# One query pass for all 256 tokens and 156 instead of 152 dense columns in a two-layer expert kernel

## The chip, the cores and the metric

The kernel runs on one core of a Trainium2 chip. TensorE (PE) multiplies matrices, VectorE (DVE), ScalarE (ACT) and GpSimd (POOL) work beside it, SyncE (SP) issues most transfers, and all transfers of the core share its 16 DMA engines. The metric is device time of one launch, in microseconds (us).

## What is computed

Two transformer blocks follow one another; each ends in a layer that retrieves experts by product keys. The change touches only this layer, which runs once in each block, for 256 tokens of 1024 features, in float32. Cut to what matters:

```
def peer_ffn(h, w_q, sub_keys, u, v):            # 256 tokens, 8 heads, 128 x 128 experts
    qh = (h @ w_q).reshape(t, 8, 2, 128)         # a query for each of 16 key lists
    s  = einsum('thcd,hcnd->thcn', qh, sub_keys) # 128 scores in each list
    s1, i1 = top_k(s[:, :, 0], 16);  s2, i2 = top_k(s[:, :, 1], 16)
    cand, cand_idx = s1 + s2, i1 * 128 + i2      # 256 candidates of a head
    top_s, pos = top_k(cand, 16)
    eidx = take_along_axis(cand_idx, pos);  g = softmax(top_s)
    coef = g * gelu(h . u[eidx])                 # 8 x 16 = 128 experts of a token
    return sum(coef * v[eidx])
```

## The kernel before

All of it is one function, `peer_layer`, called for layer 1 and for layer 2. It treats its 256 tokens in three ways. The first 96 (GATHERED) are handled by gathering: POOL fetches, for 128 (token, pick) pairs at a time, 128 rows of `in_uv` (the expert's u and v side by side, 8 KB a row, 1.05 MB a gather) into one of four buffers of `expert_rows`; DVE multiplies them with the token (L1402, the dot) and adds v times a coefficient (L1410, the add), and ACT makes the coefficient in between (L1284, L1286). The next 8 tokens (SHARED) are gathered too, but each is spread over 16 partitions. That makes 96 + 8 = 104 gathers in a layer. The other 152 tokens are dense: PE computes all 16384 experts for them, 128 steps "up" (L1138, step e multiplies 128 experts' u with all dense tokens) and 128 steps "down" (L1163, v times coefficients), and the coefficients of experts that a token didn't pick are zero. Each step is 8 float32 products, which PE executes as 16 passes, over 128x152 data, and needs one tile of 128x1024 weights (0.524 MB).

The order inside a layer is written out by hand on every engine:

- **Queries.** PE makes the 16 query tiles for tokens 0 to 127 (`query`, L1105), then all scores of these tokens (`score`, L1117), then both for tokens 128 to 255. ACT copies every result out of PSUM (L1296 queries, L1251 scores). The query weights pass through the ring twice.
- **Choice.** `select(tt)` on DVE finds the best 16 of each list (L1434 to L1451), pairs them up and finds the best 16 of a head, and looks up the experts. `select(0)` ends in `listed`: from then on POOL may gather. `select(1)`, for the second half of the tokens, is interleaved with the first gathered pairs, one at each call of `early`; EARLY_PAIRS = 18 of them.
- **Gates.** The dense tokens' picks and weights reach PE as one-hot matrices: `choice(tt)` transposes the picks on PE (L1147, after the up steps named in CHOICE_AFTER), DVE makes one-hots (`one_hots`, L1521), ACT weighs them (`weigh_hots`, L1270), PE multiplies (`group`, L1155), four tokens a group, 38 groups, the first after up step GATES_FROM = 54. Before that up step `work` still holds queries and lists.
- **Pairs later on.** From GATES_FROM on, DVE does 4 pairs for 7 up steps (`pairs_by`). In the down steps POOL waits for PE: gather p, from the fifth that is left on, waits for down step 13 * (p - late - 4) // 5 (`late` is the number of pairs done in the up steps, 60).
- **Weights.** SP fills a ring of 8 tiles (`refill`): a tile is loaded as soon as PE has consumed the one in its place. Twelve up tiles (AHEAD_UPS) are loaded ahead during the queries into memory that isn't used yet (`load_ahead`), so that the ring has less to bring while the first pairs are gathered.

PE also waits for ACT by count: up step e needs the copy of step e-4 out of PSUM (`geld`). ACT runs in the order of up steps, and at certain steps it does something for another engine first, and waits for that: the softmax's exponentials after the steps in EXP_AFTER, the list for the spread tokens at step SHARED_LISTED, and the coefficient of early pair p after step EARLY_AFTER[p].

Of the kernel before, what the change touches and what calls it, by code (L numbers as in the profile page):

```python
# [17 lines left out]
U32 = mybir.dt.uint32  # L18
# [28 lines left out]
GATHERED, SHARED = 96, 8  # L47
# [20 lines left out]
AHEAD_UPS = (6, 12, 17, 21, 24, 27, 30, 33, 36, 39, 42, 45)  # L68
# [33 lines left out]
def plan():  # L102
# [3 lines left out]
    for name, chunks in (("in1", 10), ("v1", 4), ("ki", 1), ("in1g", 8), ("projab", 4), ("out1", 4), ("wq1", 8), ("keys1", 1), ("wq1", 8), ("keys1", 1),  # L106
                         ("uv1", 0), ("in2", 14), ("in2g", 4), ("glu", 1), ("ssmout", 2), ("mlout", 4), ("out2", 4),
                         ("wq2", 8), ("keys2", 1), ("wq2", 8), ("keys2", 1), ("uv2", 0)):
        PHASE[name] = len(LOADS)
        if chunks:  # L110
            at = DENSE_AT.setdefault(name, NDENSE)
            for c in range(chunks):
# [847 lines left out]
def peer_layer(k, layer, gelu, gate, gain, shift, out=None):  # L960
# [8 lines left out]
    PASS = PH + 1  # L969
# [9 lines left out]
    pairs_by = lambda e: EARLY_PAIRS + 4 * max(0, e - GATES_FROM) // 7  # L979
# [4 lines left out]
    with ExitStack() as ctx:  # L984
# [6 lines left out]
        best_i = sb("best_index", [P, NC2, PK], U32)  # L991
        pos = sb("top_pos", [P, PH, PK], U32)
        whole = sb("picked_int", [P, P], I32)
        replica = rows[:, BUFFERS - 1, 0:D].rearrange("p (k t) -> p k t", k=KD)
# [31 lines left out]
        best, best_f = above(NC2, PK), above(NC2, PK)  # L1026
# [33 lines left out]
        with nc.Block() as block:  # L1060
            @block.sync
            def _(sp):
                def load_ahead(c):
                    if c < AHEAD:
                        sp.dma_start(ahead_tile(c), k.args["ut" + layer][AHEAD_UPS[c], :, :]).then_inc(k.ahead_loaded[c], 16)

                refill(k, sp, 2 * PASS + NR + NB, None,
                       [(k.tile_ready, 2 * c + 2) for c in range(PH)] + [(k.scored, 4)]
                       + [(k.tile_ready, NC2 + 2 * c + 2) for c in range(PH)] + [(k.scored, 8)]
# [9 lines left out]
            def _(pool):  # L1079
                pool.wait_ge(k.listed.sem, k.listed.at(1))  # L1080
                for p in range(NP):
                    if p >= BUFFERS:
                        pool.wait_ge(k.added.sem, k.added.at(p - BUFFERS + 1))
                    if p > late + BUFFERS:
                        pool.wait_ge(k.w_used.sem, k.w_used.at(13 * (p - late - BUFFERS) // 5))
                    if p == BUFFERS - 1:
# [8 lines left out]
            def _(pe):  # L1095
                def query(tt, c):

                    if c % 2 == 0:
                        arrived(k, pe, PASS * tt + c // 2)
                    w = chunk(k, PASS * tt + c // 2).rearrange("p (k n) -> p k n", k=KD)  # L1100
                    pe.wait_ge(k.act_emptied.sem, k.act_emptied.at(NC2 * tt + c - 3))
                    for kk in range(KD):
                        if c == 0:
                            pe.wait_ge(normed.sem, normed.at(KD * tt + kk + 1))
                        ins = nc.tensor.matmul(k.bank[c % 4][:, 0:P], w[:, kk, (c % 2) * P:(c % 2 + 1) * P],  # L1105
                                               k.h[:, kk, tt * P:(tt + 1) * P], start=kk == 0, stop=kk == KD - 1)
                    ins.then_inc(k.tile_ready.sem, 1)

                def score(tt):

                    arrived(k, pe, PASS * tt + PH)
                    keys = chunk(k, PASS * tt + PH).rearrange("p (c n) -> p c n", n=NKEYS)
                    for q in range(4):
                        pe.wait_ge(k.act_emptied.sem, k.act_emptied.at(NC2 * tt + 4 * q + 4))
                        pe.wait_ge(k.keyed.sem, k.keyed.at(4 * (tt - 1) + q + 1))
# [1550 lines left out]
```

## Time and profile before

| | |
|---|---|
| median of 3 runs | 2004.68 us (2001.94 to 2007.39) |
| the profiled execution | 2011.07 us, of which 2009.3 us span |
| expert layer 1 in the trace | from 301.3 us (first query) to 981.4 us (last down step) |
| expert layer 2 in the trace | from 1327.6 us to 1999.9 us |
| busy share of the span | PE 94%, DVE 63%, ACT 23% |
| moved by DMA | 621.72 MB, mean 309 GB/s |

The two layers are 1352 us of the span. A busy PE is not a PE at its peak: matmuls are pipelined, and a step that waits for its weights shows as a short gap and a somewhat longer step. The trace's times are counted from the start of the span; T0 below is the start of a layer's first query.

### The profile page before, as it was taken

Reading aid. Unit: us, or ns where it says so; the run is one execution under the profiler, and the core shown is the slowest. Engines: PE = TensorE matmul, PEld = TensorE weight load, DVE = VectorE, ACT = ScalarE, POOL = GpSimd, SP = SyncE. Lnnn points to the kernel's source line nnn. Section 1 sums busy time; section 2 is a strip of 40 time slices with the busy share of each in tenths; the row PEclk is TensorE's granted clock in tenths of the full one; section 3 lists DMA queues with packets and bytes.
Section 4 is the critical chain, followed back from the end, with each engine's and each line's share of the span. In section 5 each row is a group of like instructions: output and inputs, shape, how many; then the busy total and the mean of one; then the engine's idle time right before and its main releaser. Section 6 shows DMA issues by size and latency. Waiting matters only on the chain. (4 is left out here: it accounts for less than half of the span.)

```text
span 2009.3 us, 32969 instructions
## 1 busy us (share of the span) xinstructions
PE 1891.4 (94%) x12953; PEld 1755.5 (87%) x12953; DVE 1262.6 (63%) x2817; ACT 468.6 (23%) x1660; POOL 377.4 (19%) x320
## 2 busy tenths in 40 slices
PE   7989999999999899999899989999999999899998
PEld 5877779999999889999888566789999999898998
DVE  6359323898898754442399973318897998544441
ACT  3003312323544300000211023013224444100010
POOL 0100000033333312210000630000333333221210
PEclk9989999999999999999999997999999999999999
DMA  7972248899999999999443120269999999999994
GB/s 301 422 272 84 85 171 349 299 413 398 409 414 415 415 413 414 409 414 352 142 144 141 64 94 0 105 247 361 371 403 401 415 415 415 414 414 415 413 403 150
DMA packets 126202, 621.72 MB, mean 309 GB/s; under 512 B 15388, under 2 KB 17596, under 8 KB 83936
## 3 DMA queue, kind: packets, MB, share of 16 engines
q1 hardware_dynamic: 90832, 379.62, 48.9%
q0 software_dynamic: 33104, 238.85, 29.0%
q8 instruction: 103, 1.69, 0.3%
q10 hardware_dynamic: 2112, 1.14, 0.2%
q14 instruction: 51, 0.42, 0.1%
HBM read 616.92 MB, written 2.62 MB: 308 GB/s over the span
## 5 line engine op out<-in xcount | busy, mean ns | idle before, releaser
L1163 PE MATMUL bank<-expert_coef,ring 128*128 128x152 f32 x4096 | 545.3, 294 | 33.8 <-DMA ring<-in_uv 30.3
L1163 PEld LDWEIGHTS bank<-expert_coef,ring 128*128 128x128 f32 x4096 | 531.8, 190 | 46.8 <-DMA ring<-in_uv 41.6
L1090 POOL DMA_INDIRECT expert_rows<-in_uv,pair_index x208 | 302.0, 1452 | 1213.4 <-DVEq L1555 458.2
L1138 PE MATMUL bank<-h,ring 128*128 128x152 f32 x3712 | 502.5, 294 | 10.8 <-DMA ring<-in_ut 10.6
L1138 PEld LDWEIGHTS bank<-h,ring 128*128 128x128 f32 x3712 | 486.3, 190 | 14.8 <-DMA ring<-in_ut 14.3
L1402 DVE CUSTOM_DVE_ANT_0 expert_rows<-expert_rows,h_tokens 128x1024 f32<-128x1024 f32 x192 | 234.3, 1220 | 170.6 <-DMA expert_rows<-in_uv,pair_index 170.4
L1410 DVE SCALAR_TENSOR_TENSOR pair_sum<-expert_rows,pair_coef,pair_sum 128x1024 f32<-128x1024 f32 x192 | 245.9, 1281 | 51.1 <-ACT pair_coef L1286 49.1
L1284 ACT ACTIVATE pair_act<-pair_dot 128x1 f32<-128x1 f32 x208 | 42.2, 203 | 593.9 <-DVE pair_dot L1402 593.8
L1105 PE MATMUL bank<-h,ring 128*128 128x128 f32 x1024 | 120.0, 282 | 6.1 <-ACT h L1293 3.8
L1105 PEld LDWEIGHTS bank<-h,ring 128*128 128x128 f32 x1024 | 119.4, 198 | 7.0 <-issue 7.0
L1270 ACT ACTIVATE work<-work,choice 128x128 f32<-128x128 f32 x304 | 96.9, 406 | 0.0
L1521 DVE TENSOR_TENSOR work<-const,choice 128x1024 f32<-128x1024 f32 x76 | 92.3, 1218 | 0.0
L1155 PE MATMUL bank<-work 128*128 128x128 f32 x608 | 82.3, 278 | 5.2 <-ACT work L1270 5.2
L1155 PEld LDWEIGHTS bank<-work 128*128 128x128 f32 x608 | 74.3, 191 | 6.9 <-ACT work L1270 6.1
L1699 PE MATMUL bank<-h,ring 128*128 128x272 f32 (+1 forms) x320 | 73.8, 395 | 6.8 <-PEq L1060 6.8
L1699 PEld LDWEIGHTS bank<-h,ring 128*128 128x128 f32 x320 | 62.1, 194 | 18.4 <-issue 7.0
L396 PE MATMUL bank<-h,ring 128*128 128x256 f32 x320 | 73.0, 390 | 2.5 <-issue 2.5
L1262 ACT ACTIVATE expert_coef<-bank 128x152 f32<-128x152 f32 (+27 forms) x254 | 62.0, 254 | 53.9 <-PE bank L1138 51.2
L396 PEld LDWEIGHTS bank<-h,ring 128*128 128x128 f32 x320 | 62.1, 195 | 13.9 <-issue 5.2
L1260 ACT ACTIVATE expert_act<-bank 128x16 f32<-128x16 f32 (+36 forms) x146 | 34.1, 234 | 156.9 <-PE bank L1138 156.6
L1980 POOL TENSOR_TENSOR mixed<-s_z,s_rot 128x256 f32<-128x256 f32 x64 | 49.1, 788 | 99.9 <-DVE s_z L1954 99.9
L1538 DVE TENSOR_TENSOR expert_coef<-expert_act,expert_coef 128x16 f32<-128x16 f32 (+36 forms) x146 | 34.1, 233 | 48.0 <-ACT expert_coef L1278 29.6
(395 smaller groups left out, 2053.6 us busy)
## 6 DMA issues: line engine op xcount, KB each, us to landing
ring<-in_uv SPq DMA_DIRECT2D x256, 512.0 KB, 14.7
ring<-in_ut SPq DMA_DIRECT2D x232, 512.0 KB, 13.3
ring<-in_dense SPq DMA_DIRECT2D x96, 1024.0 KB, 4.9
ada<-in_ada POOLq DMA_DIRECT2D x16, 1024.0 KB, 17.4
expert_coef<-in_ut SPq DMA_DIRECT2D x24, 512.0 KB, 8.2
ada<-in_ada SPq DMA_DIRECT2D x8, 1024.0 KB, 23.1
expert_rows<-in_uv,pair_index POOLq DMA_INDIRECT x208, 9.9
bias_rows<-proj_t POOLq DMA_DIRECT2D x1, 1536.0 KB, 6.5
```

What stands on the lines that cost most here:

```text
L396: return nc.tensor.matmul(k.bank[j % BANKS][:, 0:TOK], w[:, kk, (j % 2) * P:(j % 2 + 1) * P], k.h[:, kk, 0:TOK], start=kk == 0, stop=kk == ...
L1090: pool.indirect_dma_start(rows[:, p % BUFFERS, :], None, table, bass.IndirectOffsetOnAxis(pindex[:, p:p + 1], 0))\
L1105: ins = nc.tensor.matmul(k.bank[c % 4][:, 0:P], w[:, kk, (c % 2) * P:(c % 2 + 1) * P], k.h[:, kk, tt * P:(tt + 1) * P], start=kk == 0, sto ...
L1138: ins = nc.tensor.matmul(k.bank[e % 4][:, 0:DENSE], w[:, kk, :], k.h[:, kk, FRONT:TOK], start=kk == 0, stop=kk == KD - 1)
L1155: ins = nc.tensor.matmul(k.bank[b][:, q * P:(q + 1) * P], second[:, g % BUF, q, :], first[:, g % BUF, q, :], start=True, stop=True)
L1163: ins = nc.tensor.matmul(down_bank(i), w[:, i * P:(i + 1) * P], A[:, e, :], start=e == 0 and i % 3 == 0, stop=e == NB - 1, skip_group_chec ...
L1262: ins = nc.scalar.activation(A[:, e, t:], k.bank[e % 4][:, t:DENSE], gelu)
L1270: ins = nc.scalar.activation(first[:, g % BUF, q, :], first[:, g % BUF, q, :], ACT.Copy, scale=k.choice[:, 2, t:t + 1])
L1402: nc.vector.tensor_tensor_reduce(u, u, htok[:, :] if p < GATHERED else hpart[:, :], 1.0, 0.0, ALU.mult, ALU.add, dots[:, p:p + 1])\
L1410: nc.vector.scalar_tensor_tensor(total[:, :], rows[:, p % BUFFERS, D:], pcoef[:, p:p + 1], total[:, :], ALU.mult, ALU.add).then_inc(k.adde ...
L1521: nc.vector.tensor_tensor(hots[:, :, g % BUF, :, :], iota.unsqueeze(1).unsqueeze(1).broadcast_to(shape), k.choice[:, 0:2, t:t + GROUP].uns ...
L1699: ins = nc.tensor.matmul(out, left, right, start=kk == 0, stop=kk == KD - 1)
```

## The change

The queries are made once for all 256 tokens (256 columns a pass; only the first tile is made in two halves), and the scores of four lists are made as soon as their queries are there. The query weights are loaded once, and the keys come by one transfer of their own. DVE finds the best of each list while PE goes on with queries, for both halves of the tokens (`lists`), so that `select` begins with the candidates. Of the spread tokens 4 remain, so a layer has 100 gathers, 156 dense columns and 39 groups. The numbers that place the other steps are new: gates from up step 37, 10 early pairs, one pair for 2 up steps after that.

```diff
-GATHERED, SHARED = 96, 8
+GATHERED, SHARED = 96, 4
-GATES_FROM = 54
-EARLY_PAIRS = 18
-EARLY_AFTER = tuple(9 + 5 * p // 2 for p in range(EARLY_PAIRS))
-EXP_AFTER = (5, 38)
-CHOICE_AFTER = (20, 55)
-SHARED_LISTED = 22
+GATES_FROM = 37
+EARLY_PAIRS = 10
+EARLY_AFTER = tuple(14 + 23 * p // 10 for p in range(EARLY_PAIRS))
+EXP_AFTER = (5, 23)
+CHOICE_AFTER = (12, 40)
+SHARED_LISTED = 13
-AHEAD_UPS = (6, 12, 17, 21, 24, 27, 30, 33, 36, 39, 42, 45)
+AHEAD_UPS = (4, 11, 15, 18, 20, 22, 24, 26, 28, 30, 32, 34)
...
-    pairs_by = lambda e: EARLY_PAIRS + 4 * max(0, e - GATES_FROM) // 7
+    pairs_by = lambda e: EARLY_PAIRS + max(0, e - GATES_FROM) // 2
...
             def _(sp):
+                sp.dma_start(rows[:, 2, :], k.args["dense"][DENSE_AT["keys" + layer], :, :]).then_inc(k.keys_dma, 16)
                 def load_ahead(c):
-                    if c < AHEAD:
+                    for i in range(2 * c, min(2 * c + 2, AHEAD)):
...
+                    for cols in (slice(0, P), slice(P, TOK)) if c == 0 else (slice(0, TOK),):
+                        for kk in range(KD):
+                            if c == 0:
+                                pe.wait_ge(normed.sem, normed.at(cols.start // P * KD + kk + 1))
+                            ins = nc.tensor.matmul(k.bank[c % 4][:, cols], w[:, kk, (c % 2) * P:(c % 2 + 1) * P],
+                                                   k.h[:, kk, cols], start=kk == 0, stop=kk == KD - 1)
...
-                for tt in range(TT):
-                    for c in range(NC2):
-                        query(tt, c)
-                    score(tt)
+                for c in range(NC2):
+                    query(c)
+                    if c == 4:
+                        pe.wait_ge(k.keys_dma, 16 * int(layer))
+                    if c % 4 == 0 and c:
+                        for n in range(c // 2 - 2, c // 2):
+                            score(n)
+                for n in range(6, 8):
+                    score(n)
...
+                def lists(n):
+                    q, tt = n // TT, n % TT
+                    cs = range(4 * q, 4 * q + 4)
+                    dve.wait_ge(k.keyed.sem, k.keyed.at(n + 1))
+                    for c in cs:
+                        ch(nc.vector.max(best[:, tt, c, 0:8], s[:, tt, c, :]))
...
                 def select(tt):
-                    for c in range(NC2):
-                        ch(nc.vector.max(best[:, c, 0:8], s[:, tt, c, :]))
-                    ch.wait()
-                    early(tt)
...
-                dve.wait_ge(k.keyed.sem, k.keyed.at(4))
+                for n in range(8):
+                    lists(n)
                 select(0)
```

Three places show how the order moves. First PE at the start of layer 1, before: the queries of one half (L1105), its scores (L1117), the other half, and the first two up steps (L1138).

```order
L1094 UNCONDITIONAL_BRANCH
L1105 MATMUL bank<-h,ring 128x128 x128
L1117 MATMUL bank<-ring,work 128x128 x16
L1105 MATMUL bank<-h,ring 128x128 x128
L1117 MATMUL bank<-ring,work 128x128 x16
L1138 MATMUL bank<-h,ring 128x152 x16
```

The same place now, with queries on L1110, scores on L1120 and up steps on L1146:

```order
L1110 MATMUL bank<-h,ring 128x128 x16
L1110 MATMUL bank<-h,ring 128x256 x32
L1120 MATMUL bank<-expert_rows,work 128x128 x8
L1110 MATMUL bank<-h,ring 128x256 x32
L1120 MATMUL bank<-expert_rows,work 128x128 x8
L1110 MATMUL bank<-h,ring 128x256 x32
L1120 MATMUL bank<-expert_rows,work 128x128 x8
L1110 MATMUL bank<-h,ring 128x256 x24
L1120 MATMUL bank<-expert_rows,work 128x128 x8
L1146 MATMUL bank<-h,ring 128x156 x16
```

Half of the scores of the first half used to be followed by another 128 products; now the last quarter of the scores of both halves stands right ahead of the up steps.

Second, DVE at the start of layer 1, before: from the last normalised feature rows to the first step after the lists (CAST), with 16 lists at a time.

```order
L1545 SCALAR_TENSOR_TENSOR h<-x,gain,choice 128x128 x8
L1434 MAX expert_coef<-expert_coef 128x8 x16
L1438 MAX_INDEX best_index<-expert_coef 128x8 x16
L1442 MATCH_REPLACE expert_coef<-expert_coef 128x128 x16
L1447 MAX expert_coef<-expert_coef 128x8 x16
L1451 MAX_INDEX best_index<-expert_coef 128x8 x16
L1455 CAST expert_coef<-best_index 128x256
```

Now the end of the same stretch: the eighth and last block of four lists, of the second half of the tokens, stands ahead of the first half's CAST.

```order
L1459 MAX_INDEX expert_coef<-expert_coef 128x8 x4
L1448 MAX expert_coef<-expert_coef 128x8 x4
L1451 MAX_INDEX expert_coef<-expert_coef 128x8 x4
L1453 MATCH_REPLACE expert_coef<-expert_coef 128x128 x4
L1456 MAX expert_coef<-expert_coef 128x8 x4
L1459 MAX_INDEX expert_coef<-expert_coef 128x8 x4
L1464 CAST expert_coef<-expert_coef 128x256
```

The first half's selection has moved behind all lists of both halves.

Third, DVE just behind `listed`, at the first early pair, before: the 16 maxima of the second half stand ahead of the pair's set-up (MEMSET, COPY) and its dot (ISA), and lists follow.

```order
L1553 COPY pair_gate<-picked 32x32 x3
L1434 MAX expert_coef<-expert_coef 128x8 x16
L1391 MEMSET pair_sum 128x1024
L1392 COPY h_tokens<-h_tokens 32x1024
L1402 ISA expert_rows,pair_dot<-expert_rows,h_tokens 128x1024
L1402 ISA pair_dot 128x1
L1438 MAX_INDEX best_index<-expert_coef 128x8 x8
```

Now, with the last of the candidate sums ahead of the set-up:

```order
L1472 TENSOR_TENSOR expert_coef<-expert_coef 128x8x8
L1402 MEMSET pair_sum 128x1024
L1403 COPY h_tokens<-h_tokens 32x1024
L1413 ISA expert_rows,pair_dot<-expert_rows,h_tokens 128x1024
L1413 ISA pair_dot 128x1
L1479 SCALAR_TENSOR_TENSOR expert_coef<-const,expert_coef 128x432
L1482 MAX expert_coef<-expert_coef 128x8 x8
```

The pairs that stood between lists are gone from there; the rest of `select(1)` has the same steps between the same ten pairs as before.

## Rows read from the trace of the kernel before

**Rows 1.** Stretches: length, busy us and instructions of each engine, clock, DMA share, GB/s.

```profile
487.90:686.90 199.00, 190.45 (x1475) 187.54 (x1475) 170.07 (x275) 93.33 (x416) 70.06 (x42) 0.99 1.01 411
686.90:917.60 230.70, 214.91 (x1617) 209.84 (x1617) 111.16 (x133) 20.88 (x84) 46.09 (x40) 1.00 1.02 413
917.60:981.40 63.80, 63.80 (x504) 63.69 (x505) 14.29 (x41) 7.49 (x22) 0.99 (x1) 1.00 0.74 264
1327.60:1412.70 85.10, 85.10 (x727) 85.10 (x728) 52.09 (x245) 22.97 (x57) 0.00 (x0) 0.98 0.87 335
1412.70:1511.10 98.40, 96.85 (x751) 96.62 (x750) 93.92 (x281) 24.55 (x92) 33.50 (x22) 1.00 1.01 401
1511.10:1707.20 196.10, 188.91 (x1475) 186.18 (x1475) 169.44 (x275) 92.99 (x416) 69.36 (x42) 1.00 1.02 411
1707.20:1941.80 234.60, 219.44 (x1633) 212.26 (x1633) 111.69 (x134) 20.89 (x84) 49.57 (x41) 1.00 1.02 414
1941.80:1999.90 58.10, 58.10 (x457) 58.10 (x458) 10.48 (x28) 4.71 (x13) 0.00 (x0) 1.00 0.62 225
```

**Rows 2.** Waits of PE in layer 2: who for whom, us, times, longest.

```profile
PE bank L1163 <- DMA ring<-in_uv: 14.9, 24, 1.4
PE bank L1138 <- DMA ring<-in_ut: 4.1, 6, 1.1
...
PE bank L1163 <- DVE expert_coef L1530: 1.5, 1, 1.5
```

**Rows 3.** Timeline of PE: start, length, instructions, idle before; queries to gates, layer 2.

```profile
1327.57 30.45 PE L1105 MATMUL bank<-h,ring 128*128 128x128 f32 x256 [2.29 <-DVE h L1545]
1357.86 3.74 PE L1117 MATMUL bank<-ring,work 128*128 128x128 f32 x32
1390.02 3.74 PE L1117 MATMUL bank<-ring,work 128*128 128x128 f32 x32
1393.59 4.30 PE L1138 MATMUL bank<-h,ring 128*128 128x152 f32 x32
1397.72 1.04 PE L1222 MATMUL bank<-const,h 128*96 128x128 f32 x8
1399.47 8.43 PE L1138 MATMUL bank<-h,ring 128*128 128x152 f32 x64
1438.74 0.49 PE L1147 MATMUL bank<-const,picked 128*128 128x128 f32 x3
1511.05 1.16 PE L1155 MATMUL bank<-work 128*128 128x128 f32 x8 [1.55 <-ACT work L1270]
1512.04 2.23 PE L1138 MATMUL bank<-h,ring 128*128 128x152 f32 x16
```

**Rows 4.** Timeline of PE: a projection in 256 columns, and layer 1's first group.

```profile
38.97 58.97 PE L396 MATMUL bank<-h,ring 128*128 128x256 f32 x272
...
487.87 1.16 PE L1155 MATMUL bank<-work 128*128 128x128 f32 x8 [1.55 <-ACT work L1270]
```

**Rows 5.** Timeline of DVE, layer 2: lists, selection, the first pair, the first one-hots.

```profile
1362.26 3.19 DVE L1434 MAX8 expert_coef<-expert_coef 128x8 f32<-128x128 f32 x16 [29.91 <-ACT expert_coef L1251]
...
1381.49 0.29 DVE L1455 CAST expert_coef<-best_index 128x256 f32<-128x256 uint32 x1
...
1409.97 0.29 DVE L1511 TENSOR_REDUCE expert_coef<-picked 128x8 f32<-128x128 f32 x1 [1.77 <-ACT picked L1321]
...
1412.05 0.59 DVE L1553 COPY pair_gate<-picked 32x32 f32<-32x32 f32 x3
...
1420.93 1.22 DVE L1402 CUSTOM_DVE_ANT_0 expert_rows<-expert_rows,h_tokens 128x1024 f32<-128x1024 f32 x1 [2.89 <-DMA expert_rows<-in_uv,pair_index]
...
1454.21 0.29 DVE L1455 CAST expert_coef<-best_index 128x256 f32<-128x256 uint32 x1
...
1505.45 3.49 DVE L1521 TENSOR_TENSOR work<-const,choice 128x1024 f32<-128x1024 f32 x3
```

**Rows 6.** Timeline of ACT, layer 2: a copy of scores.

```profile
1358.95 0.60 ACT L1251 ACTIVATE expert_coef<-bank 128x512 f32<-128x512 f32 x1 [0.62 <-PE bank L1117]
```

More of the change, by code:

```diff
@@ L111, in plan @@
             at = DENSE_AT.setdefault(name, NDENSE)
-            for c in range(chunks):
+            for c in range(chunks if name[:4] != "keys" else 0):
                 LOADS.append(("dense", at + c, unit, 2))
@@ L990, in peer_layer @@
         index = sb("expert_index", [P, TT, P], I32)
-        best_i = sb("best_index", [P, NC2, PK], U32)
         pos = sb("top_pos", [P, PH, PK], U32)
         whole = sb("picked_int", [P, P], I32)
+        keys = rows[:, 2, :].rearrange("p (c n) -> p c n", n=NKEYS)
         replica = rows[:, BUFFERS - 1, 0:D].rearrange("p (k t) -> p k t", k=KD)
@@ L1095, in _, with query @@
             def _(pe):
-                def query(tt, c):
+                def query(c):
                     if c % 2 == 0:
[L1099 to L1106, printed above, removed]
-                    ins.then_inc(k.tile_ready.sem, 1)
@@ L1109, in score @@
[L1109 to L1115, printed above, removed]
-                        for c in range(4 * q, 4 * q + 4):
-                            ins = nc.tensor.matmul(k.bank[4 + q][:, (c % 4) * P:(c % 4 + 1) * P],
-                                                   qt[:, c, tt * P:(tt + 1) * P], keys[:, c, :], start=True, stop=True)
-                        ins.then_inc(k.scored.sem, 1)
@@ new lines, in query, with score @@
+                    ins.then_inc(k.tile_ready.sem, 1)
+                def score(n):
+                    q, tt = n // TT, n % TT
+                    pe.wait_ge(k.act_emptied.sem, k.act_emptied.at(4 * q + 4))
+                    pe.wait_ge(k.keyed.sem, k.keyed.at(n - 3))
+                    for c in range(4 * q, 4 * q + 4):
+                        ins = nc.tensor.matmul(k.bank[4 + n % 4][:, (c % 4) * P:(c % 4 + 1) * P],
+                                               qt[:, c, tt * P:(tt + 1) * P], keys[:, c, :], start=True, stop=True)
+                    ins.then_inc(k.scored.sem, 1)
@@ L1293, in _ @@
                         nc.scalar.activation(h, h, ACT.Identity, bias=shift[:, kk:kk + 1]).then_inc(normed.sem, 1)
-                    for c in range(NC2):
-                        act.wait_ge(k.tile_ready.sem, k.tile_ready.at(NC2 * tt + c + 1))
-                        nc.scalar.activation(qt[:, c, tt * P:(tt + 1) * P], k.bank[c % 4][:, 0:P], ACT.Copy)\
-                            .then_inc(k.act_emptied.sem, 1)
-                    for n in range(4 * tt, 4 * tt + 4):
-                        scores(n)
+                for c in range(NC2):
+                    act.wait_ge(k.tile_ready.sem, k.tile_ready.at(c + 1))
+                    nc.scalar.activation(qt[:, c, :], k.bank[c % 4][:, 0:TOK], ACT.Copy).then_inc(k.act_emptied.sem, 1)
+                    if c % 4 == 0 and c:
+                        for n in range(c // 2 - 2, c // 2):
+                            scores(n)
+                for n in range(6, 8):
+                    scores(n)
                 act.wait_ge(normed.sem, normed.at(KD))
@@ L1445, in select @@
-                    ch.wait()
-                    for c in range(NC2):
-                        ch(nc.vector.max(best[:, c, 8:16], s[:, tt, c, :]))
-                    ch.wait()
-                    early(tt)
-                    for c in range(NC2):
-                        ch(nc.vector.max_index(best_i[:, c, 8:16], best[:, c, 8:16], s[:, tt, c, :]))
-                        if c % 8 == 7:
-                            early(tt)
-                    ch.wait()
-                    ch.then(nc.vector.tensor_copy(best_f, best_i[:, :, :]))
@@ L1633, in _ @@
                 scale_out(back, 2, 0)
-    k.tile_ready.advance(TT * NC2)
-    k.act_emptied.advance(TT * NC2)
+    k.tile_ready.advance(NC2)
+    k.act_emptied.advance(NC2)
     for sig in {scaled, normed}:
```

63 lines of the change are left out of this document (36 added, 27 removed).

## The prediction

> **What bounds the kernel now.** I read the stretches of the two expert layers first, then PE's waits, then the timelines of PE and DVE at the start of layer 2. From a layer's first group on, the 16 DMA engines are full: they move 411 GB/s in the up steps and 413 to 414 in the down steps, at a share of 1.01 to 1.02, and it makes no difference that PE's gaps look small [rows 1]. PE waits for ring tiles 19.0 us in layer 2 [rows 2], and steps that follow such a wait are longer too: until the last gather has landed, 102 down steps take 234.6 us, 2.30 each, where a step that waits for nothing takes 2.07 (4.13 us for 32 passes, 129.1 ns a pass [rows 3]). After that PE runs alone: 58.1 us for 26 steps and 4.4 us of sums; the DMA engines move 225 GB/s there [rows 1]. So a layer has three parts. In the opening (T0 to the first group: 183.5 us in layer 2, 186.6 in layer 1 [rows 3, 4]) DVE's selection sets when gathers may begin; the DMA engines are not full there, 335 GB/s until `listed` and 401 after it. In the middle the end is set by bytes. In the tail PE sets it.
>
> **What the change takes away and adds, by parts.**
>
> *Queries.* A pass over 256 columns takes 58.97 / 272 = 216.8 ns [rows 4]; 256 such passes are 55.5 us, where 512 passes over 128 columns took 30.3 + 28.6 (the first half loses 1.7 us at its start) [rows 3]. The scores are the same 64 passes, 2 x 3.57. PE's new wait for the last query's copy, with no scores left to cover it, is about 0.6, the length of a score copy [rows 6]. Sum 55.5 + 7.1 + 1.7 + 0.6 = 64.9 us against 66.0 before: one microsecond. The 9.4 MB of weights and keys that aren't loaded a second time are saved in a stretch of 335 GB/s, where no engine waits for them [rows 1]; I cost that at nothing. In between (4 lists' scores every 14 us) DVE works on lists while it used to wait 29.9 us [rows 5].
>
> *Listing.* Before, it began when the first half's scores were there, with the other half's queries still to come. Now scores 6 and 7 come last. Score 6 is ready at 64.0, copied at 64.7 [rows 6]; two blocks of four lists, at 19.2 us for sixteen [rows 5], are 9.6: CAST at T0 + 74.3. From CAST to the end of listing took 31.15 us, of which 1.77 waited for the exponentials [rows 5], which ACT made in the order of up steps; now ACT waits for DVE there, so 29.4 remain. `listed` comes at **T0 + 103.7 instead of 85.1**, and `choice(0)`, 1.8 us ahead of it, at 101.9. PE stands at that transposition after up step 12, at 64.9 + 1.75 (the other transposes) + 13 x 2.12 = 94.2: it waits some 7.7 us, where before the picks had been there for 28 us (1438.7 against 1410.8, which is the 1409.97 and the three short steps from there [rows 3, 5]). Behind it on PE stand all further up steps. The ring is full then, so the DMA engines stop too.
>
> *Gates.* From the second half's CAST to its first one-hots DVE took 52.4 us with ten pairs in between (1454.2 to 1505.4 + 1.2 [rows 5]); the change leaves this stretch as it is but for the first pair, which now has its set-up (0.8 more than an add) and must wait for the first gather. A gather landed 8.3 us after listing, and DVE waited 2.9 for it; now 0.9 us less stands ahead of it, so 3.8 [rows 5]. One-hots at 103.7 + 0.2 + 52.4 + 4.6 = 160.9, weighed on ACT in 1.2: first group at **T0 + 162 instead of 183.5**. PE would be there at 64.9 + 1.75 + 38 x 2.12 + 0.3 = 147.5 if nothing held it, so 14.5 us of waits for DVE lie in the opening in all, ACT's stops for the early pairs' coefficients among them. This cost is bounded by 0 (PE alone sets it) and some 19 (lists and waits 4 us longer).
>
> *What is left at the first group.* 38 up steps are done instead of 55. A gather needs the buffer that the add four pairs earlier frees; with nine adds done, 13 have been issued, instead of 22 (POOL's count until 1511.1 [rows 1]). The change saves 4 gathers a layer, but 87 are left instead of 82. The last one now waits for down step 13 x 40 / 5 = 104 instead of 101.
>
> *Wider steps.* From 129.1 ns at 152 columns to 216.8 at 256 is 0.843 ns a column; four more make 132.5, and a step 2.12 instead of 2.07. That is 0.054 x 256 = 14 us a layer on PE, and one more group (0.99, 1511.05 to 1512.04 [rows 3]). In the middle the wider steps hide behind the DMA engines (2.30 us a step); if that cover goes, they cost what rival 1 says. Eight pairs less on DVE and POOL cost nothing: neither sets the middle.
>
> **The sum.** Layer 2, middle before: 411 x 196.1 + 414 x 234.6 = 177.7 MB in 430.7 us, 412.6 GB/s. Now 17 + 3 tiles more at 0.524 MB (10.5) and 5 gathers more at 1.05 (5.2): 193.4 MB, 468.8 us at that rate. Last landing 162 + 468.8 = 630.8 (before 614.2). Tail: 23 steps x 2.12 + 4.4 = 53.2. End at T0 + 684.0 against 672.3: **+11.7**. Layer 1: first group at 163 (its first group was 3.1 us later than layer 2's; the second half's own wait for its features goes, so I leave one); 177.1 + 15.7 = 192.8 MB at 412.1 GB/s, 467.8; tail 24 steps (27 before) x 2.12 + 8.0 = 58.9; end at 689.7 against 680.1: **+9.6**. Together +21.3 us. The profiled execution took 2011.07 and would take 2032; it lies 6.4 above the median, to which I add the same: 2004.7 + 21.3 = **2026**.
>
> The sum hangs on the rate of the full DMA engines, and the rows put it at 411 to 414 GB/s, under a demand of 437 to 449 (a tile of 0.524 MB for each step and 1.05 MB for each gather: 4 gathers for 7 up steps and their 38 groups, 5 for 13 down steps, at the lengths of rows 3). The Trainium skill, "DMA: Bandwidth & Descriptors", section Bandwidth, puts the fabric's ceiling at 435 GB/s and a large single-core copy at 425. By 435 the 193.4 MB would take 445 us, PE would set the middle and rival 1's time would come out; by this case's rows it doesn't.
>
> **Rivals.**
>
> *1. Faster: the DMA engines no longer bind.* If the tiles arrive whenever PE wants them, layer 2 ends at 162 + 90 x 2.12 + 39 x 0.99 + 1.5 [rows 2] + 128 x 2.12 + 4.4 = T0 + 668.7 (-3.6) and layer 1 at 673.3 (-6.8): 2004.7 - 10 = **1994**, between 1986 and 2001. For it: with one pair for two up steps the up steps ask for 1.05 MB in 2.12 + 0.43 x 0.99 = 2.54 us, 413 GB/s, no more than the engines gave, while before it was 1.12 MB in 2.57, 437. Against it: the down steps still ask for 0.524 + 1.05 / 2.6 = 0.928 MB in 2.12 us, 437 GB/s, and have gotten 414 [rows 1]. It decides from a rate of 437 on, or if the ring carries a lead through 104 down steps. Chance 0.22.
>
> *2. The opening is shorter than I add up.* If PE is held only at `choice(0)` (the first gather lands sooner with fewer bytes in flight, and DVE's selection keeps ahead of the early pairs), the first group comes at some 155.5 in each layer, and the sum is 13 smaller: **2013**, between 2005 and 2016. For it: DVE's waits in that stretch were few [rows 5]. Against it: DVE's steps there are one chain whose lengths are all in the trace. Chance 0.22.
>
> *3. Worse than my sum.* A wait makes PE's clock fall: the granted clock is 0.98 (nearly all at its upper level, 2.4 GHz, the rest at 1.2) in the stretch in which the queries start behind 2.3 us of idleness, and the first half's passes lost 1.7 us there [rows 1, 3]; two waits of 4 to 8 us a layer could cost 2 us each, and the DMA engines idle meanwhile when the ring is full. That adds up to 8: **2034** and above. Chance 0.06. The Trainium skill, "TensorE: Matmul & The Clock Gate", section "HAM oscillation — how this bites in real kernels", warns of idle gaps between bursts of matmuls, after which the next burst starts at the lower clock; the queries' row agrees.
>
> That the change doesn't do what it says is excluded by the order of the instructions.
>
> **How the numbers follow.** Chances: my forecast (2016 to 2034) 0.50, rival 1 0.22, rival 2 0.22, rival 3 0.06. 0.3% (6 us) is about what a measurement of this kernel can tell from no change. Faster by more: 0.19, from rival 1. Within: 0.12, the edges of rivals 1 and 2. Slower by more: 0.69, the rest. Range: 1994 to 2037; below it lies about half of rival 1, above it part of rival 3. The forecast's own range is 2016 to 2034, from the bounds of the opening (4 us a layer either way).
>
> **What would show it.** Right: `listed` (POOL's first gather) near T0 + 104; PE waits at the first transposition of picks for 5 to 10 us and again ahead of the first group, near T0 + 162; 410 to 415 GB/s from there to the last gather; 2.25 us or more a down step until then, 2.12 after it; layers of 684 and 690 us. The queries end at T0 + 65. Wrong: down steps at 2.12 from the start with the DMA share below 1 (rival 1), a first group before T0 + 157 (rival 2), or gathers that start before T0 + 95.

## The result, and the profile after

| | before | after |
|---|---|---|
| median, us | 2003.64 (2001.94 to 2007.39, 4 runs) | 2023.56 (2022.56 to 2025.93, 4 runs) |
| ratio to before | | 1.0099, 95% interval 1.0080 to 1.0117 |
| layer 1: first group, end (us from T0) | 186.6, 680.1 | 161.3, 687.9 |
| layer 2: first group, end (us from T0) | 183.5, 672.3 | 161.6, 685.5 |
| between layer 1's end and layer 2's T0, us | 346.2 | 340.3 |
| all bytes moved, MB | 621.72 | 594.39 |

"End" is the start of the layer's last sums on PE; here its last down step ends there. The change costs 19.9 us by the medians. (One run of before, 2002.60 us, came later than the table ahead of the prediction; the profiled execution of before, 2011.07 us, is not among the four.) By the two profiled executions the expert layers take 7.8 and 13.2 us more, 21.0 in all; the rest of the traces differs by 9.6 us the other way (before's profiled run was 3.7 us longer ahead of layer 1 and 5.9 between the layers, and lay 7 us above its median), so spans alone would show only 11.5.

The stretches of layer 2 after, in the columns of [rows 1] (length; busy time and instructions of PE, weight loads, DVE, ACT, POOL; clock; DMA share; GB/s): queries and lists, selection, up steps, down steps to the last stall, and the tail.

```profile
1325.90:1431.10 105.20, 96.08 (x568) 88.99 (x569) 73.17 (x373) 22.05 (x47) 0.00 (x0) 0.94 0.57 206
1431.10:1487.50 56.40, 53.52 (x398) 53.28 (x396) 53.26 (x127) 14.21 (x52) 19.10 (x13) 0.98 0.94 353
1487.50:1716.10 228.60, 228.58 (x1755) 227.94 (x1755) 183.23 (x303) 103.55 (x459) 74.95 (x45) 0.99 1.01 406
1716.10:1956.10 240.00, 227.21 (x1664) 221.45 (x1664) 114.62 (x137) 21.69 (x87) 49.03 (x41) 1.00 1.02 413
1956.10:2011.40 55.30, 55.26 (x425) 55.26 (x426) 10.41 (x28) 4.68 (x12) 0.94 (x1) 1.00 0.58 208
```

Multiply length by rate. The opening of before moved 85.1 x 0.335 + 98.4 x 0.401 = 68.0 MB in 183.5 us [rows 1]; the new one moves 21.7 + 19.9 = 41.6 MB in 161.6 us. Behind the first group there were 190.8 MB before and there are 203.4 now (92.8 + 99.1 + 11.5). The layer moves 13.8 MB less, but the opening gave up 26.4 MB: 12.6 MB more stand behind it, where the engines are full. That is the change in two numbers: an opening 21.9 us shorter, and 12.6 MB, 30.5 us at 413 GB/s, more behind it. The other 4.6 of layer 2's 13.2 us are, in this account, room left unused there: the tail moves 208 instead of 225 GB/s, and the up steps 406 instead of 411. This is bookkeeping and doesn't yet show a cause; the experiments test it.

PE's waits in layer 2 (who for whom; us in total, times, longest), to be laid beside [rows 2]:

```profile
PE bank L1171 <- DMA ring<-in_uv: 11.7, 16, 1.4
PE bank L1155 <- DVEq L1523: 8.4, 1, 8.4
PE bank L1163 <- ACT work L1279: 2.9, 1, 2.9
```

No up tile is waited for any more, down tiles still are. The wait of 8.4 us at the choice is new, and the one ahead of the first group has grown from 1.55 us [rows 3] to 2.9. Their place, from the timelines of PE, POOL and DVE (start, length, instructions, idle before and who ended it):

```profile
1429.20 0.90 PE L1155 MATMUL bank<-const,picked 128*128 128x128 f32 x3 [8.45 <-DVEq L1523]
1429.89 5.95 PE L1146 MATMUL bank<-h,ring 128*128 128x156 f32 x32
...
1487.49 1.96 PE L1163 MATMUL bank<-work 128*128 128x128 f32 x8 [2.88 <-ACT work L1279]
...
1956.14 36.31 PE L1171 MATMUL bank<-expert_coef,ring 128*128 128x156 f32 x272 [0.74 <-DMA ring<-in_uv]
```

```profile
1431.25 1.11 POOL L1094 DMA_INDIRECT expert_rows<-in_uv,pair_index  x1 [202.74 <-DVEq L1565]
```

```profile
1401.50 0.29 DVE L1464 CAST expert_coef<-expert_coef 128x256 f32<-128x256 uint32 x1
...
1430.32 0.59 DVE L1563 COPY pair_gate<-picked 32x32 f32<-32x32 f32 x3
...
1437.13 1.23 DVE L1413 CUSTOM_DVE_ANT_0 expert_rows<-expert_rows,h_tokens 128x1024 f32<-128x1024 f32 x1 [1.74 <-DMA expert_rows<-in_uv,pair_index]
```

PE stands 8.45 us at the transposition of the picks (until T0 + 103.3), `listed` comes when DVE's last copy for the pairs (L1563) ends, at T0 + 105.0, the first gather goes out at T0 + 105.4, the first group is there at T0 + 161.6 and the last stall ends at T0 + 630.3.

### The profile page after: what moved, and what is told of

Its sections match the earlier page's. It is cut to its first block and busy times, and to the rows that moved or that the text cites. A ratio compares the mean times of both kernels' runs of the same rounds, so it can differ in the third digit from the quotient of the medians.

```text
span 2020.8 us, 32075 instructions
## 1 busy us (share of the span) xinstructions
PE 1905.9 (94%) x12489; PEld 1763.4 (87%) x12489; DVE 1256.5 (62%) x2831; ACT 469.6 (23%) x1654; POOL 364.7 (18%) x312
## 2 busy tenths in 40 slices
DMA packets 122439, 594.39 MB, mean 294 GB/s; under 512 B 14956, under 2 KB 17164, under 8 KB 83504
## 5 line engine op out<-in xcount | busy, mean ns | idle before, releaser
L1171 PE MATMUL bank<-expert_coef,ring 128*128 128x156 f32 x4096 | 557.7, 298 | 24.8 <-DMA ring<-in_uv 21.7
L1171 PEld LDWEIGHTS bank<-expert_coef,ring 128*128 128x128 f32 x4096 | 544.8, 190 | 36.9 <-DMA ring<-in_uv 34.1
L1146 PE MATMUL bank<-h,ring 128*128 128x156 f32 x3712 | 516.3, 298 | 0.0
L1094 POOL DMA_INDIRECT expert_rows<-in_uv,pair_index x200 | 289.2, 1446 | 1249.9 <-DVEq L1565 488.0
L1146 PEld LDWEIGHTS bank<-h,ring 128*128 128x128 f32 x3712 | 503.0, 192 | 0.0
L1110 PE MATMUL bank<-h,ring 128*128 128x256 f32 (+1 forms) x544 | 115.2, 373 | 5.8 <-ACT h L1302 3.3
L1110 PEld LDWEIGHTS bank<-h,ring 128*128 128x128 f32 x544 | 100.3, 193 | 19.0 <-issue 5.8
L1547 DVE TENSOR_TENSOR expert_coef<-expert_act,expert_coef 128x4 f32<-128x4 f32 (+29 forms) x180 | 41.7, 237 | 90.5 <-ACT expert_coef L1287 74.2
L1269 ACT ACTIVATE expert_act<-bank 128x4 f32<-128x4 f32 (+29 forms) x180 | 42.5, 236 | 215.3 <-PE bank L1146 211.8
L1271 ACT ACTIVATE expert_coef<-bank 128x156 f32<-128x156 f32 (+38 forms) x252 | 59.3, 249 | 34.8 <-PE bank L1146 34.8
```

The source lines that it names most:

```text
L1094: pool.indirect_dma_start(rows[:, p % BUFFERS, :], None, table, bass.IndirectOffsetOnAxis(pindex[:, p:p + 1], 0))\
L1110: ins = nc.tensor.matmul(k.bank[c % 4][:, cols], w[:, kk, (c % 2) * P:(c % 2 + 1) * P], k.h[:, kk, cols], start=kk == 0, stop=kk == KD - 1)
L1146: ins = nc.tensor.matmul(k.bank[e % 4][:, 0:DENSE], w[:, kk, :], k.h[:, kk, FRONT:TOK], start=kk == 0, stop=kk == KD - 1)
L1171: ins = nc.tensor.matmul(down_bank(i), w[:, i * P:(i + 1) * P], A[:, e, :], start=e == 0 and i % 3 == 0, stop=e == NB - 1, skip_group_chec ...
L1271: ins = nc.scalar.activation(A[:, e, t:], k.bank[e % 4][:, t:DENSE], gelu)
```

## The experiments

First group and end are from T0 of the layer in the profiled run, in us; the medians and the ratios are to the kernel before, which ran beside each. In runs 4, 9 and 10 PE waits ahead of a layer's last sums (2.2, 2.0 and 6.4 us in layer 1, 3.9 us in layer 2 of run 10), and the end includes that wait.

| run | median | ratio, 95% | layer 1: first group, end | layer 2: first group, end |
|---|---|---|---|---|
| 1 choice later on PE | 2025.97 | 1.0110, 1.0087 to 1.0133 | 162.8, 688.3 | 162.6, 685.3 |
| 2 8.4 MB more in the opening | 2027.62 | 1.0123, 1.0093 to 1.0152 | 161.8, 687.1 | 162.1, 685.3 |
| 3 changed, pace 14/5 | 2011.57 | 1.0040, 1.0026 to 1.0055 | 161.5, 680.3 | 161.5, 676.8 |
| 4 before, pace 15/5 | 1984.53 | 0.9921, 0.9893 to 0.9949 | 184.0, 666.5 | 183.6, 662.1 |
| 5 before, 156 columns | 2009.11 | 1.0022, 1.0005 to 1.0038 | 189.4, 681.1 | 186.5, 675.3 |
| 6 changed, 152 columns | 2026.43 | 1.0104, 1.0075 to 1.0134 | 161.4, 687.0 | 161.3, 683.4 |
| 7 last lists behind the choice | 2020.12 | 1.0079, 1.0054 to 1.0105 | 159.7, 687.8 | 160.0, 680.8 |
| 8 before, choice held back | 2063.83 | 1.0299, 1.0258 to 1.0340 | 213.0, 706.6 | 212.6, 702.1 |
| 9 changed, run 7 and pace 29/10 | 2001.97 | 0.9990, 0.9968 to 1.0011 | 160.1, 677.1 | 159.6, 671.8 |
| 10 before, pace 31/10 | 1996.24 | 0.9958, 0.9943 to 0.9973 | 186.9, 678.0 | 183.6, 664.0 |

The theory under test is the prediction's: from the first group on the end is set by bytes, then by the steps that are left when the gathers are over. Its rivals: PE's new waits are the cost, or the wider steps are, and what the DMA engines do is incidental.

**Is it the width?** Each half of the change alone. Run 5, the kernel before in 156 columns (the edit also gives the tile `best_index` another place in memory, which isn't shown):

```diff
-GATHERED, SHARED = 96, 8
+GATHERED, SHARED = 96, 4
...
```

> The kernel before with 4 instead of 8 tokens spread over partitions: 156 columns in every up and down step, 100 instead of 104 gathers a layer, and the opening of before (two passes of queries, lists after them). Its last gather waits for down step 91 instead of 101. Theory (the end is the last landing and the steps left behind it; 4.2 MB less at 412 GB/s lands 10 us earlier in a layer, while ten more steps are left then, and a step is 0.05 us longer): about +3 us a layer, time 2006 to 2012 us. Rival (the width itself is what the change costs: 232 up and 256 down steps of 16 matmuls a layer, PE bound, at 2.12 instead of 2.07 us): +13 to 15 us a layer, time about 2031 us.

Measured 2009.11 us, 4.2 above the kernel before beside it: the layers end 1.0 and 3.0 us later. 3.0 us of that is the opening, whose 55 up steps are 0.054 us longer each (first group +2.8 and +3.0); behind it nothing is lost. Run 6, the changed kernel in 152 columns (three of the tiles loaded ahead are other ones, since the layout in memory goes with the width):

```diff
-GATHERED, SHARED = 96, 4
+GATHERED, SHARED = 96, 8
-AHEAD_UPS = (4, 11, 15, 18, 20, 22, 24, 26, 28, 30, 32, 34)
+AHEAD_UPS = (1, 8, 14, 18, 20, 22, 24, 26, 28, 30, 32, 34)
```

> The changed kernel with 8 tokens spread instead of 4: 152 columns in every step, 104 instead of 100 gathers a layer, with the short opening. Its last gather waits for down step 114 instead of 104. Theory (bytes up to the last landing, then the steps left): 4.2 MB more in a layer land 10 us later, ten steps fewer are left behind that, each step 0.05 us shorter: about +1 us a layer, time 2021 to 2028 us. Rival (the width is the cost of the change): 14 to 15 us a layer less, time about 1994 us.

Measured 2026.43 us, where the width as the cost asked for 1994. Its layers end 0.9 and 2.1 us earlier than the changed kernel's. In layer 2 PE is busy for 650.00 us, 10.6 less than in the changed kernel, but it stands idle 8.5 us more. Its waits in the whole run say for what:

```profile
PE bank L1171 <- DMA ring<-in_uv: 33.2, 47, 2.1
PE bank L1155 <- DVEq L1523: 17.7, 2, 8.9
PE bank L1163 <- ACT work L1279: 10.2, 4, 3.9
```

Narrower steps and four more gathers: waits for down tiles rise from 21.7 to 33.2 us (waits of both layers). So at the pace of these kernels the cost is in the single pass with its opening, not in the four tokens that go from gathers to columns: by the medians the single pass costs 21.6 us in 152 columns and 14.5 in 156, while the four tokens cost 4.2 us on the kernel before and gain 2.9 on the changed one. (The two runs move columns and 4.2 MB of gathers a layer together, as the change does; columns alone were not run.) This is the more telling because PE's busy time misleads: in layer 2 it is 648.40 us before and 660.64 after, a difference of 12.2 that nearly fits the 13.2 by itself.

**Is it bytes, and where they are moved?** Run 2 loads 8 unused blocks of weights a layer while the queries are computed:

```diff
+                for i in range(8):
+                    pool.dma_start(rows[:, BUFFERS - 1, :], k.args["dense"][DENSE_AT["wq" + layer] + i, :, :]).then_inc(k.extra_dma, 16)
+                    pool.wait_ge(k.extra_dma, 16 * (8 * int(layer) - 7 + i))
...
+                act.wait_ge(k.extra_dma, 16 * 8 * int(layer))
```

> The changed kernel with 8 more loads of 1.05 MB in each layer (17 MB in all, of data that nothing uses), issued and landed while the queries are computed, when the DMA engines are lightly used. Theory (bytes cost only where the engines are saturated, from the first group on): first group and last stall stay within 2 us of the changed kernel's T0+161.6 and T0+630.3, time 2022 to 2027 us. Rival (every byte counts wherever it is moved, 8.4 MB at 412 GB/s in a layer): 20 us a layer, time about 2064 us.

The engines took them: the stretch of the queries and lists in layer 2 rose from 206 to 293 GB/s.

```profile
1326.30:1429.00 102.70, 94.12 (x560) 87.23 (x560) 71.46 (x365) 21.53 (x46) 3.72 (x7) 0.97 0.77 293
```

Both layers end within 0.8 us of the changed kernel's. The last stalls come at T0 + 624.1 and 625.8, further from the changed kernel's than the 2 us that I gave, and the ends don't follow them. The median, 2027.62, is 4 us above the changed kernel's and 0.6 above my range, but the four runs spread over 7.6 us. Nowhere near 2064: 17 MB more in the two openings cost next to nothing. That the 12.6 MB a layer behind the first group are what the change pays for is not shown by this run; the next ones bear on it.

Run 3 moves no byte more or less; it lets the gathers of the down steps go later:

```diff
-                        pool.wait_ge(k.w_used.sem, k.w_used.at(13 * (p - late - BUFFERS) // 5))
+                        pool.wait_ge(k.w_used.sem, k.w_used.at(14 * (p - late - BUFFERS) // 5))
```

> The changed kernel with its gathers let go later: gather p waits for down step 14(p-c)/5 instead of 13(p-c)/5, so the last one waits for step 112 instead of 104; the same bytes and the same work. Theory (bytes saturate the engines up to the last landing, and the end is that landing and the steps that are left then, 2.12 us each): fewer steps are left behind the last landing, 6 to 7 us less in a layer, time 2009 to 2012 us, with PE's waits for ring tiles or gathered rows no larger than before. Rival (PE itself is the bound and its 11.7 us of waits for the ring are incidental): the time stays at 2023 to 2025 us.

Measured 2011.57 us, 12.0 below the changed kernel; the layers end 7.6 and 8.7 us earlier. Up steps, down steps to the last stall, tail of layer 2:

```profile
1485.10:1713.00 227.90, 227.90 (x1753) 227.51 (x1754) 183.24 (x303) 103.42 (x459) 75.02 (x45) 0.99 1.01 406
1713.00:1951.50 238.50, 230.88 (x1717) 227.68 (x1716) 108.89 (x131) 20.68 (x83) 47.47 (x40) 1.00 1.02 414
1951.50:2000.40 48.90, 48.90 (x377) 48.90 (x378) 16.19 (x35) 5.68 (x16) 1.87 (x2) 1.00 0.63 250
```

92.5 + 98.7 + 12.2 = 203.4 MB behind the first group, as after. The down steps still run at 414 GB/s. The last stall ends at T0 + 627.9 instead of 630.3, PE has done three more steps by then, and the tail, in which the engines are at 0.63, is 6.4 us shorter. PE's waits for down tiles fell from 21.7 to 14.3 us in both layers. (The layers gained 16.3 us together and the median 12.0; the rest of the profiled execution was some 5 us longer.)

**How far does that go, and on which kernel?** Run 4 is the kernel before at a pace of 15/5, run 10 at 31/10:

```diff
-        FLIP_AFTER, TOTAL_AFTER = NB - 8, NB - 5
+        FLIP_AFTER, TOTAL_AFTER = NB - 6, NB - 3
-                        pool.wait_ge(k.w_used.sem, k.w_used.at(13 * (p - late - BUFFERS) // 5))
+                        pool.wait_ge(k.w_used.sem, k.w_used.at(15 * (p - late - BUFFERS) // 5))
```

> The kernel before with its gathers let go later: gather p waits for down step 15(p-c)/5 instead of 13(p-c)/5, so the last one waits for step 117 instead of 101, and the two orders of the last blocks are put 2 blocks later to match. Theory (saturated bytes up to the last landing, then the steps that are left): 12 to 13 us less in each layer, time 1978 to 1981 us, ratio 0.988. Rival A (PE alone is the bound, its waits incidental): no change, 2003 us. Rival B (gathered rows now arrive late, PE waits for each of the last gathers): slower than 2004 us, with waits of PE or VectorE for gathered rows in the second half of the down steps.

Measured 1984.53 us, the fastest of all, 19 us below the kernel before and 39 below the changed one, though 3.5 us above the range that I gave: 12 to 13 us were expected of each layer, and layer 1 gained 13.6, layer 2 10.2. Of layer 1's gain 2.6 us lie in its opening (184.0 against 186.6), ahead of all that was changed, so the pace gave some 10 to 11 us a layer. In layer 2 the engines are now full nearly to the end:

```profile
1494.50:1690.00 195.50, 188.26 (x1465) 185.15 (x1466) 167.77 (x270) 92.47 (x412) 68.35 (x41) 1.00 1.02 411
1690.00:1955.60 265.60, 258.07 (x1964) 254.24 (x1962) 116.85 (x141) 22.12 (x90) 46.25 (x42) 1.00 1.02 413
1955.60:1973.00 17.40, 17.02 (x137) 16.84 (x138) 7.64 (x24) 3.93 (x10) 0.00 (x0) 1.00 0.12 50
```

80.4 + 109.7 + 0.9 = 190.9 MB, the 190.8 of before, in 478.5 us instead of 488.8. At this pace a step asks for 0.524 MB of ring and 0.350 of a gather (1.05 in 3 steps), 0.874 MB, which is 2.12 us at 413 GB/s, close to the 2.07 that PE needs.

For run 10 the two lines read `31 * (p - late - BUFFERS) // 10` and `NB - 4, NB - 1`.

> The kernel before with gather p let go at down step 31(p-c)/10, the last at step 120 instead of 117 in the run at 15/5 and 101 in the kernel before, and the two orders of the last blocks 2 blocks later than there. Theory (at 15/5 PE waits about 6 us a layer for down tiles, which a slower pace takes away, but the last gathered rows are then added only about 6 us later, and the norm of the next layer behind them is exposed): no gain left, 1980 to 1989 us against 1984.5 us. Rival (bytes still press everywhere): 5 to 6 us a layer less, about 1974 us.

Measured 1996.24 us, 12 above run 4 and 7 above the upper end that I gave. Rival and theory both gave too short a time. The tail of layer 1 on PE, and the last gather on DVE:

```profile
955.44 3.58 PE L1182 MATMUL bank<-const,extra_sum 128*128 128x8 f32 x16 [3.70 <-DVE extra_sum L1410]
958.87 7.97 PE L1163 MATMUL bank<-expert_coef,ring 128*128 128x152 f32 x48
966.68 1.85 PE L1170 MATMUL bank<-picked,ones 128*128 128x16 f32 x16
968.38 3.80 PE L1170 MATMUL bank<-work,ones 128*128 128x104 f32 x32
978.55 6.31 PE L1170 MATMUL bank<-work,ones 128*128 128x152 f32 x32 [6.37 <-DVE work L1627]
```

```profile
952.27 1.23 DVE L1402 CUSTOM_DVE_ANT_0 expert_rows<-expert_rows,h_shared 128x1024 f32<-128x1024 f32 x1 [5.26 <-DMA expert_rows<-in_uv,pair_index]
```

The last gathered rows reach DVE 5.26 us after it is free, PE waits 3.70 us for their sum and 6.37 us for the norm behind it (2.21 in run 4): 10 us in the layer that does this norm for the next one. (3 us more lie in its opening, which has a clock of 0.98 against 1.00 in run 4; the profiled execution of before has the same 0.98 there, and the same length.) The bytes of the end are then no longer the limit; the chain behind the last gather is.

Run 9 gives the changed kernel the same treatment: the edit of run 7 below, `29 * (p - late - BUFFERS) // 10` (last gather at step 116) and `NB - 6, NB - 3`.

> The changed kernel with two edits together: the lists of the last half block behind the first choice (as in the run that did this alone, -3.4 us), and gather p let go at down step 29(p-c)/10 instead of 13(p-c)/5, the last at step 116 instead of 104, with the two orders of the last blocks 2 blocks later. It answers whether the change pays once the bytes no longer press. Theory (both gains add until PE is the bound; then the change still has its 4 more columns in every step and PE's waits in the opening): 4 more steps than at 14/5 give 6 us, the list 3.4 us, so 2000 to 2005 us, 16 to 21 us above the kernel before with the same treatment (1984.5 us). Rival (the change is worth its shorter opening once bytes are out of the way): 1984 us or less.

Measured 2001.97 us: no slower than the kernel before, 17.4 us slower than run 4. (Its profiled execution took 2014.37 us, 12 above the median; the surplus lies between the layers, so the layers can be compared.) PE now waits little for tiles, 9.7 us in both layers:

```profile
PE bank L1171 <- DMA ring<-in_uv: 9.7, 11, 1.4
...
PE bank L1155 <- DVEq L1523: 6.7, 2, 3.4
PE bank L1163 <- ACT work L1279: 6.6, 2, 3.3
PE bank L1146 <- ACT expert_coef L1271: 4.5, 4, 2.5
```

So the change doesn't pay once bytes press less either. Layer 2 as a whole, run 9 and then run 4:

```profile
1331.30:2003.00 671.70, 656.17 (x4806) 646.24 (x4807) 434.54 (x966) 166.04 (x657) 141.86 (x100) 0.99 0.92 365
1310.90:1973.00 662.10, 645.40 (x5039) 638.05 (x5040) 437.41 (x959) 165.46 (x660) 147.37 (x104) 1.00 0.97 391
```

PE is busy 10.8 us more in run 9, and the layer is 9.6 us longer: what the change costs there goes with PE's time. That the wider steps are most of it (14 us a layer by the prediction's term) is argued and not shown, because the changed kernel in 152 columns was not run at a slower pace. At the pace of 13/5 fewer columns don't free it: run 6, with its last gather at step 114 already, is held by bytes in layer 2's down steps until its last stall, at T0 + 652.1. Behind its first group:

```profile
1491.80:1716.00 224.20, 221.86 (x1729) 220.18 (x1730) 180.25 (x298) 101.15 (x450) 73.60 (x45) 0.99 1.01 408
1716.00:1982.50 266.50, 248.80 (x1861) 241.41 (x1860) 126.16 (x153) 24.42 (x99) 58.36 (x47) 1.00 1.02 413
1982.50:2013.90 31.40, 31.40 (x249) 31.30 (x250) 10.51 (x28) 4.71 (x13) 0.00 (x0) 1.00 0.50 197
```

These are 207.7 MB, and the run takes 2026 us. So the change sits between two limits, and the kernel before lies lower on both: the bytes behind the first group (190.8 MB against 203.4 in 156 columns and 207.7 in 152), and PE's busy time in layer 2 (648.4 us against 660.6 and, by little, 650.0).

**The opening.** Run 1 asks whether PE's 8.45 us are the cost:

```diff
-CHOICE_AFTER = (12, 40)
+CHOICE_AFTER = (17, 40)
```

> The changed kernel with PE's choice of the first token class put behind 17 instead of 12 of the up steps it does ahead of the first group, so that PE no longer reaches it 8.45 us before VectorE has the index. Theory (the first group is set by VectorE's chain and the layer's end by the bytes): the wait of 8.45 us before the choice goes, PE waits about as much longer for the first group's work, the first group stays at T0+161 to 163, the last stall at T0+628 to 632, and the time is 2021.5 to 2025.5 us, ratio to the kernel before 1.009 to 1.011. Rival (PE's own idle 8.45 us in each of the two layers is what the change costs): the time falls by 17 us to about 2007, ratio 1.0015.

Measured 2025.97 us, half a us above my range, nothing gained. The last stall of layer 2 came at T0 + 615.0, not at 628 to 632, and the layer still ended at 685.3, as in run 2: the last stall alone doesn't fix the end. And the run tells less than I wanted: PE's idle time was not removed, it moved to the up steps behind the choice. ACT, which empties their banks, stands in its own order behind the same picks:

```profile
1435.59 2.36 PE L1146 MATMUL bank<-h,expert_coef 128*128 128x156 f32 x16 [0.95 <-ACT expert_coef L1271]
1443.20 3.85 PE L1146 MATMUL bank<-h,ring 128*128 128x156 f32 x16 [5.25 <-ACT expert_coef L1271]
```

It shows that the wait's place on PE doesn't matter, and that the first group follows DVE's chain (162.6 and 162.8), not PE's. Run 7 shortens that chain:

```diff
-                for n in range(8):
+                for n in range(7):
...
+                lists(7)
```

> The changed kernel with the lists of the last half block made behind the first token class's choice instead of ahead of it on VectorE, so that the first choice is ready 4 to 5 us earlier. Theory (the first group is set by VectorE's chain behind the choice, of which the wait for the first gathered rows takes a part back): choice at T0+98 to 99, first group 1.5 to 2.5 us earlier, time about 2020 us (2017 to 2023). Rival A (listing sets the end one for one, 4.9 us a layer): about 2013.5 us. Rival B (an opening that is shorter is taken back by the bytes): first group earlier but the end unchanged, 2023 to 2025 us.

Choice 5 us earlier, first group 1.6 us earlier, median 3.4 us lower, as the theory had it; the wait at the choice fell to 3.38 us. The intervals of run 7 and of the changed kernel overlap, and the layers gained 0.1 and 4.7 us, so the sign is likely and the size is not settled: layer 1's end is what rival B said, layer 2's is nearly what rival A said. Run 8 lengthens the chain on the kernel before:

```diff
-                dve.wait_ge(k.keyed.sem, k.keyed.at(4))
+                dve.wait_ge(k.keyed.sem, k.keyed.at(8))
```

> The kernel before with the first choice held back until all eight half blocks have been listed, instead of four: VectorE starts it about 32 us later, and nothing else is changed. Theory (the engines carry few bytes until the first group, so a later first group moves all bytes behind it): first group 26 to 32 us later, the end 20 to 29 us later in each layer, time 2045 to 2062 us. Rival (the opening's length is taken back, since PE uses the time for up steps and the bytes behind the first group become fewer): first group later by as much, the end within 5 us, time 2000 to 2014 us.

First group 26.4 and 29.1 us later, the ends 26.5 and 29.8 us later, 2063.83 us. One for one, more than the 20 to 29 that I gave for the end: PE stands in the meantime, because the up steps ahead of the first group are a fixed number in its order.

```profile
423.75 8.40 PE L1138 MATMUL bank<-h,ring 128*128 128x152 f32 x48 [14.06 <-ACT expert_coef L1262]
```

That is the difference to the change under study. Run 8 changes the length of the opening and leaves the work behind it alone, and the end follows one for one (the median, 2063.83, is 1.8 us above my range). The change shortens the opening by taking work out of it (17 up steps and their tiles), and the end comes later.

## Why the prediction was right

2026 was forecast, +21.3 us; 2023.56 came, +19.9, and +21.0 in the two layers. Step by step, layer 2 if nothing else is said:

| step | forecast | trace |
|---|---|---|
| queries end | T0 + 64.9 | 65.4 |
| CAST | 74.3 | 75.6 |
| `listed` | 103.7 | 105.0 |
| first gather | 104 | 105.4 |
| PE's wait at the choice | 7.7 | 8.45 |
| DVE's wait for the first gather | 3.8 | 1.74 |
| first group | 162 | 161.6 |
| first group, layer 1 | 163 | 161.3 |
| gathers issued by then | 13 | 13 |
| last stall ends | 630.8 | 630.3 |
| the same, layer 1 | 630.8 | 629.0 |
| tail | 53.2 | 55.2 |
| end | 684.0 | 685.5 |
| end, layer 1 | 689.7 | 687.9 |

The sum is closer than its parts, and that is luck: layer 1 lost 7.8 us where 9.6 were forecast, layer 2 13.2 where 11.7 were.

*The opening* was right within 2.1 us at each step, by lengths from [rows 3, 5] alone. Two small misses cancel: `listed` comes 1.3 us later (the last two blocks of lists start 0.6 later and take 0.7 longer; from the CAST on it took 29.4 us, as forecast), and DVE waits 2.1 us less for its rows, perhaps because fewer bytes are in flight.

*The middle* was right in its sum and wrong in two of its terms. 193.4 MB at 412.6 GB/s were forecast; 191.9 MB came at 409.5, and each is worth some 3.5 us, in opposite directions. The lower rate is that of the up steps, 406 GB/s, outside the 410 to 415 that was to show the forecast right. There PE is busy 228.58 of 228.60 us and waits for no tile, as rival 1 had said of this stretch (90 steps and 39 groups, 229.4 us by its terms). So the middle as a whole was not set by bytes: its up steps were PE's, at the edge of what the engines give, and its down steps were the engines' (413 GB/s, 240.0 us where 104 steps of 2.12 are 220.5). Rival 1 fell in the down steps alone, where I had put the demand at 437 GB/s, and that was worth the 17 us between its 668.7 and the end.

*The tail*: 55.2 against 53.2, because 24 steps were left behind the last stall and not 23. Run 3 shows what this part is: not work that is left over by chance, but the price of gathers that are over too early.

*Queries*: the single pass saved 0.6 us of PE where 1.1 was forecast, and the bytes that it saves, costed at nothing, were worth next to nothing (run 2, from the other side).

*Rivals 2 and 3*: no first group came before T0 + 157; the clock did fall to 0.94 in the stretch with the wait (the two up steps behind it took 5.95 us, where such a pair took 4.41), which is inside my 2 us.

What stays open: whether the changed kernel in 152 columns would gain at a slower pace, how run 7's 5 us on DVE are shared out behind the first group, and why the stretch between the layers takes 340 us in some executions and 355 in the profiled run 9, whose clock there is 0.91 (0.95 in the profiled run of the changed kernel), with the same instructions.

## What to carry to other kernels

When the DMA engines are full in one stretch and not in the next, ask of each edit not how many bytes it saves but out of which stretch it takes them: here the kernel moves 13.8 MB a layer less and is slower: 26.4 MB left a stretch that had room, and half of them came back where there was little or none. A prefetch that runs ahead of need in a full stretch leaves an empty tail behind it; pace it so that ring and gathers together ask for just what the engines give (here one gather in 3 steps, worth 19 us on the kernel before), and stop where the chain behind the last one shows. And PE's busy time that grows by as much as the span is no proof that PE is the bound: undo the growth (run 6), and see whether the waits take it back.

## What the runs showed of the hardware

- The rate of the full engines hardly moves: 413 to 414 GB/s in the down steps of all the kernels above, whether rings ask for much or the gathers do, and at a share of 1.02. The up steps of the changed kernel show a share of 1.01 at 406, with PE waiting for no tile; a share of 1 alone doesn't say that anyone waits.
- A wait of 8.45 us on PE is followed by two up steps in 5.95 us instead of 4.41; the granted clock is 0.62 over the wait, 0.72 over the 6.8 us behind it, and 1.00 before and after (1.00 is the upper of the clock's two levels, 2.4 GHz; the others are means of that and 1.2 GHz). A wait of 14.06 us (run 8) is followed by three steps in 8.40 instead of 6.36, one of 9.88 (run 8) by two in 6.86 instead of 4.30, and one of only 3.38 (run 7) by two in 6.76 instead of 4.41. So a stall of 3.4 to 14 us costs PE 1.5 to 2.6 us more than itself, and the shorter ones not less.
